# 1 - a of a stick-breaking attention sweep on VectorE: one tensor and two constants, or a column of ones minus a tensor

## The reference, cut to what matters

```python
z = einsum('bqhd,bkhd->bhqk', q, k) * (SB_HEAD_DIM ** -0.5) + bias
log_keep = where(vis, log_sigmoid(-z), 0.0)
after = cumsum(log_keep, axis=3, reverse=True) - log_keep
a = where(vis, exp(log_sigmoid(z) + after), 0.0)
o = einsum('bhqk,bkhd->bqhd', a, v)
```

## Time and profile before

| what | value |
|---|---|
| median of 3 runs | 2906.96 us (2906.63 to 2909.41) |
| the profiled execution, its own time | 2908.15 us |
| its span, first to last instruction | 2906.3 us |
| prompt attention, first scores to last gate | 1737 to 2397 us of the span |
| mean granted clock of TensorE | 0.932 |

### The profile page before, as it was taken

One profiled execution on the slowest core, in us unless ns is written; L12 is line 12 of the kernel. 1 busy time (PEld: TensorE's weight loads), 2 busy tenths in 40 slices (PEclk: granted clock), 3 DMA queues, 4 the chain that ended last, 5 costly groups with the idle time before them and its releaser, 6 DMA issues. The chain is left out here.

```text
span 2906.3 us, 37872 instructions
## 1 busy us (share of the span) xinstructions
PE 2503.2 (86%) x14073; PEld 1568.7 (54%) x14073; DVE 1422.4 (49%) x1669; ACT 813.6 (28%) x1746; POOL 1021.5 (35%) x546
## 2 busy tenths in 40 slices
PE   5999899998599996999999667878888876886998
PEld 3555444443244443888888654555555554553443
DVE  1111066576100002555555319999999983442333
ACT  2222031223000001222222115656565642221110
POOL 2434010101000001435444005898898970002554
PEclk9999899999799997999999758999898998997999
DMA  5232212220522102011011121000000008994332
GB/s 155 90 96 92 47 30 45 61 60 15 93 64 70 59 31 65 27 39 43 29 43 33 46 99 64 30 30 1 30 30 1 30 1 291 330 325 164 127 127 83
DMA packets 150639, 224.91 MB, mean 77 GB/s; under 512 B 15632, under 2 KB 86241, under 8 KB 145416
## 3 DMA queue, kind: packets, MB, share of 16 engines
q1 hardware_dynamic: 150536, 223.50, 24.7%
HBM read 154.55 MB, written 68.91 MB: 77 GB/s over the span
## 5 line engine op out<-in xcount | busy, mean ns | idle before, releaser
L1561 DVE TENSOR_TENSOR_SCAN f_x<-f_x 128x2064 f32<-128x2064 f32 (+15 forms) x128 | 473.0, 3696 | 4.4
L1588 POOL TENSOR_TENSOR f_a<-f_a,f_x 128x2063 f32<-128x2063 f32 (+15 forms) x128 | 398.8, 3124 | 124.9 <-DVE f_x L1561 124.9
L629 PE MATMUL ps<-hT,wa 128*128 128x512 f32 (+1 forms) x960 | 354.4, 532 | 45.3 <-DMA wa<-w_in 45.3
L447 PE MATMUL ps<-hT,wc 128*128 128x512 f32 (+1 forms) x960 | 355.4, 532 | 12.8 <-DMA wc<-w_in 12.8
L629 PEld LDWEIGHTS ps<-hT,wa 128*128 128x128 f32 x960 | 168.7, 191 | 230.6 <-issue 185.1
L1456 PE MATMUL ps<-con,f_a 128*128 128x128 f32 x1216 | 189.7, 296 | 102.1 <-POOL f_a L1588 102.1
L447 PEld LDWEIGHTS ps<-hT,wc 128*128 128x128 f32 x960 | 169.1, 192 | 198.3 <-issue 198.3
L2010 PE MATMUL ps<-m_w,m_mT 128*128 128x512 f32 x544 | 238.1, 596 | 0.0
L321 PE MATMUL ps<-wt,hT_now 128*128 128x512 f32 x544 | 237.7, 595 | 0.0
L1511 ACT ACTIVATE f_at<-ps 128x512 f32<-128x512 f32 (+3 forms) x352 | 182.2, 539 | 197.6 <-PE ps L1456 195.2
L1456 PEld LDWEIGHTS ps<-con,f_a 128*128 128x128 f32 x1216 | 139.9, 149 | 138.7 <-POOL f_a L1588 108.7
(11 more groups left out here) (277 smaller groups left out, 3514.6 us busy)
## 6 DMA issues: line engine op xcount, KB each, us to landing
j_kp<-cache_k SPq DMA_DIRECT2D x128, 256.0 KB, 4.1
j_v<-cache_v SPq DMA_DIRECT2D x128, 256.0 KB, 4.7
chan<-y SPq DMA_DIRECT2D x12, 1088.0 KB, 6.0
chan<-ya SPq DMA_DIRECT2D x12, 1088.0 KB, 4.8
d_ld<-chan SPq DMA_DIRECT2D x16, 768.0 KB, 5.3
h_rows<-hg SPq DMA_DIRECT2D x17, 512.0 KB, 4.9
m_hh<-h_rows SPq DMA_DIRECT2D x17, 512.0 KB, 5.0
xin<-x_prompt SPq DMA_DIRECT2D x16, 512.0 KB, 4.1
```

What stands on the lines that cost most here:

```text
L447: m = pe.matmul(ps[:, ci, 0:n], wc[k][:, c, :], hT[:, c, c0:c0 + n], start=(c == 0), stop=(c == KC - 1))
L629: m = pe.matmul(ps[:, ci, 0:n], wc[k][h % 2][:, c, :], hT[:, c, c0:c0 + n], start=(c == 0), stop=(c == KC - 1))
L1561: dve.tensor_tensor_scan(dst[:, ::-1], dst[:, ::-1], dst[:, ::-1], 1.0, ALU.mult, ALU.bypass).then_inc(scanned, 1)
L1588: pool.tensor_tensor(w, w, x_at(u, h, i)[:, 1:], ALU.mult).then_inc(weighed, 1)
```

## The change

In place of `a * (-1) + 1` with two constants, VectorE subtracts `a` from a column of ones that is repeated along the keys, a `tensor_tensor`. The column is a new tile of one element per partition, filled ahead of the loop. The semaphore `kept` becomes two, one for each head, counted accordingly, and the waits on `filled` count one step more.

```diff
-    z_acc, z_read, kept, scanned, weighed = p.sem("z_acc"), p.sem("z_read"), p.sem("kept"), p.sem("scanned"), p.sem("weighed")
+    z_acc, z_read, scanned, weighed = p.sem("z_acc"), p.sem("z_read"), p.sem("scanned"), p.sem("weighed")
+    kept = [p.sem("kept_first_head"), p.sem("kept_second_head")]
...
+        one = sb("one", P, 1)
...
-            pe.wait_ge(filled, START + 2)
+            pe.wait_ge(filled, START + 3)
...
             dve.memset(v[:, 0, :], 0.0).then_inc(filled, 1)
+            dve.memset(one[:, :], 1.0).then_inc(filled, 1)
             dve.tensor_copy(eye[:, :], p.ident)
             dve.tensor_copy(hide[:, :], p.con[:, C_NM:C_NM + P]).then_inc(filled, 1)
+            dve.wait_ge(filled, START + 3)
...
-                        m = 4 * u + 2 * i + h
+                        m = 2 * u + i
+                        dst = x_at(u, h, i)
                         if u >= 2 and i == 0 and h == 0:
                             dve.wait_ge(weighed, START + 4 * (u - 1))
                         dve.wait_ge(z_read, START + 2 * n - 1 + h)
-                        dst = x_at(u, h, i)
-                        dve.tensor_scalar(dst, a_at(u, h, i)[:, M0:], -1.0, 1.0, ALU.mult, ALU.add).then_inc(kept, 1)
-                        dve.wait_ge(kept, START + m + 1)
+                        dve.tensor_tensor(dst, one[:, 0:1].broadcast_to([P, row_width(r)]), a_at(u, h, i)[:, M0:], ALU.subtract).then_inc(kept[h], 1)
+                        dve.wait_ge(kept[h], START + m + 1)
                         dve.tensor_tensor_scan(dst[:, ::-1], dst[:, ::-1], dst[:, ::-1], 1.0, ALU.mult, ALU.bypass).then_inc(scanned, 1)
```

## The result

The changed kernel takes 2981.93 us in the median of 4 runs (2980.36 to 2982.86), the kernel before 2906.80 beside it: 1.0256 times as long, 95% interval 1.0239 to 1.0274, 75 us more. The profiled execution has a span of 2981.0 us against 2906.3.

The account below looks back on a forecast made before the run. VectorE's stream in prompt attention, taking turns with GpSimd, was taken to bound the kernel. The longer form of 1 - a adds 76.9 us to 2906.96, giving 2984 us, range 2964 to 3002; the forecast got 0.87.

Parts of the forecast that it names:

- The bound: Prompt attention: VectorE's stream of 643.6 us sets the end; its busy time includes waits for GpSimd, as the two take turns.
- the sum: Prompt attention's work without waits: tensor_scalar 90 us, scans 305, weighings 274, gates 29; together 698 against a stream of 643.6.
- the handovers: Switches between VectorE and GpSimd, where one instruction's start lies beside the other's end, 0.14 us; said to hide 54 us.
- The price: 1 - a in prompt attention: tensor_tensor 1.306 us on average against 0.705 for tensor_scalar; 76.9 us more over 128.
- neither bound of the range: 2964 if the new form's fixed part came to lie under GpSimd's end; 3002 if it lost the 0.14 us of cover.
- The Trainium skill's estimate: 1 - a: same fixed part for both forms, per-element part halved for tensor_scalar alone; 73.6 us more in sum.
- The turns: 1 - a beside GpSimd's weighings: with two SBUF operands it still takes turns, like line 970; none of 77 us covered.
- One sign that I named: GpSimd's idle time before its weighings (line 1588) should grow in the changed profile; no size given.
- The rest: Memset of the column, TensorE's wait for it and the split semaphore kept: covered by existing waits, nothing added.
- The faster one: Rival, 0.08: the column is no second SBUF operand, so 1 - a runs beside weighings; 2817, or 2834 with nine tenths covered.
- The much slower rival: Rival, 0.03: the repeated column costs 1 - a a second pass per element, 158 us on top, about 3142.
- the one of no change: Rival, 0.02: the builder turns the constant column back into a tensor_scalar; 2907 us.

## Why the prediction was right

- **The bound.** That VectorE's stream sets the stage, with waits for GpSimd inside its busy time, held: the stream grew by 72.7 us and the end by 74.7. Waits in the scans came out as such when their second operand moved to PSUM. Their size was off: the sum priced a scan by its 2.16 ns per element with no fixed part, 305 us, which left 473.0 - 305 = 168 for waits; alone the scans take 314, and the waits are 158. So what the handovers hide is 63 us and not 54. The forecast does not feel this, as the scans are the same in both kernels.
- **The price.** Predicted 2.31 us alone at 2064 elements, measured 2.31 and 2.28; at 144 elements 0.28 instead of 421 - 112 x 1.044 = 304 ns. The mean is 1.28 us, not 1.306, so the difference is 0.575 us and 128 of them are 73.6 us, not 76.9. The sum was 3 us high: line 986, from which I took the fixed part, takes 421 ns for 256 elements, and the new form's own line through 0.28 and 2.28 us gives 0.397 there. The stream grew by 72.7, so neither bound of the range came: the new form hands over like the old one. The Trainium skill's estimate, 73.6, was the better one: by VectorE: DVE Perf Modes, section "The TRN2 errata", both forms have the same fixed part, and the trace agrees (2.28 us less 1.21 is 1.07, against 1032 cycles or, as an estimate by that page, 1.075 us).
- **The turns.** Line 970 was the right row: 249.3 us of line 1563, less 164 of its own, are 85 us of waits, and `tensor_scalar` had 175.9 - 90 = 86. None of the extra time was covered. One sign that I named did not show: GpSimd's idle time before its weighings hardly grew (124.9 to 126.1). Its waits lie in its busy time, like VectorE's, as the growth of weighings and gates shows.
- **The rest.** Semaphores, memset and waits cost nothing: 1.0007 (0.9997 to 1.0017) with only the form undone.
- **The rivals.** The faster one needed the column of ones not to count; it counts in `tensor_tensor`, and in the scan. Its mechanism is real where the column lies in PSUM, and its price, 2834, was then too good by some 40 us: I covered nine tenths of each subtraction without looking at which row's weighing is due beside which row's subtraction, and when it starts. The Trainium skill's SBUF — State Buffer, section "Who interferes with whom", says that, outside the two-port modes, an instruction with one SBUF input leaves GpSimd free, and one with two contends with a GpSimd instruction that reads SBUF; the runs agree in both directions (163.4 us with one, 249.3 with two, beside weighings that read SBUF). The much slower rival falls with 2.28 us at 2064 elements, and the one of no change with records that say `TENSOR_TENSOR`.

## What to carry to other kernels

When two engines look busy, take the shortest duration of each instruction and see what its busy time holds beyond that: here a third of the scans' 473 us was waiting for another engine, and the idle column showed none of it. For an instruction of VectorE beside one of GpSimd, look at where its operands lie before its length: moving an operand that is not even used to PSUM was worth 5% (though `tensor_scalar` took turns with its one operand in SBUF), while the choice between two forms of 1 - a was worth 2.6% the wrong way. An edit that lengthened work inside such turns cost its full length here, whatever the engine's share on the profile's page.

## What the runs showed that I had not expected

A scan whose two operands are the same tile still counts as two operands: 472.4 us against 314.0 with the unused one in PSUM. The mean granted clock of TensorE in the stage rose from 0.87 to 0.99 once it stood waiting less, and its busy time fell from 551 to 472 us with the same matrix work. As an estimate from these figures, 472 us at 0.99 would be 537 at 0.87, more than the 492 us that the stage took.
